# Moving the operands of a split-precision transformer kernel inside SBUF, and gating its merge stages in place

## The reference, cut to what matters

```python
# first stack, per layer: h = modulated rms_norm(x)
qa, ka, va, qb, kb, vb, ga, gb = split_in_proj(h @ w_in[l])
ya = window_attention_latent(...); yb = full_attention_latent(...)
m = jax.nn.sigmoid(ga) * (ya @ w_pa) + jax.nn.sigmoid(gb) * (yb @ w_pb)
x = x + gt1 * (m @ w_o)
x = x + gt2 * ((jax.nn.silu(h2 @ w_gate) * (h2 @ w_up)) @ w_down)
# second stack, per layer: three branches (sparse latent, stick-breaking, mLSTM)
proj = jnp.einsum('bsgc,gcd->bsgd', branches, w_branch)
gates = jax.nn.sigmoid(merge.reshape(bsz, seq, N_BRANCHES, D_MODEL))
x = x + jnp.sum(gates * proj, axis=2) @ w_out
```

## Time and profile before

| what | value |
|---|---|
| median of 3 runs | 2070.12 us (2069.21 to 2071.9) |
| the profiled execution's own time | 2063.66 us |
| its span, first to last instruction | 2062.2 us |
| TensorE matmul busy | 1955.9 us (95%) |
| VectorE busy | 1073.1 us (52%) |
| ScalarE busy | 873.6 us (42%) |
| GpSimd busy | 311.3 us (15%) |
| mean granted TensorE clock | 0.979 |

### The profile page before, as it was taken

One profiled execution on the slowest core, in us unless ns is written; L12 is line 12 of the kernel. 1 busy time (PEld: TensorE's weight loads), 2 busy tenths in 40 slices (PEclk: granted clock), 3 DMA queues, 4 the chain that ended last, 5 costly groups with the idle time before them and its releaser, 6 DMA issues.

```text
span 2062.2 us, 30759 instructions
## 1 busy us (share of the span) xinstructions
PE 1955.9 (95%) x12540; PEld 1617.4 (78%) x12540; DVE 1073.1 (52%) x2021; ACT 873.6 (42%) x1520; POOL 311.3 (15%) x149
## 2 busy tenths in 40 slices
PE   6999999999999999989989999899999899999996
PEld 3765676868888888677889999888788898788986
DVE  4335655642111111347776556569547755864675
ACT  3213545433222222334555444446454544755452
POOL 0220222434444443310000000000000000000100
PEclk9999999999999999999999999899999999999998
DMA  8333311243223222633237565443333444232441
GB/s 339 138 134 109 133 62 52 85 176 138 92 87 107 93 92 82 235 121 128 80 132 247 174 201 172 149 138 108 133 113 123 144 150 163 97 132 103 133 134 52
DMA packets 76700, 272.28 MB, mean 132 GB/s; under 512 B 8208, under 2 KB 11536, under 8 KB 76560
## 3 DMA queue, kind: packets, MB, share of 16 engines
q1 hardware_dynamic: 74656, 266.37, 37.6%
q10 hardware_dynamic: 1904, 3.94, 0.5%
HBM read 269.23 MB, written 1.05 MB: 131 GB/s over the span
## 4 chain that ended last, share of the span: by engine, by line
PE 82%; DVE 7%; ACT 6%; issue 2%; DMA 2%; POOL 1%; SPq 0%; ACTq 0%; DVEq 0%
PE bank L891 23%; PE bank L893 21%; PE bank L892 21%; DVE low L1671 2%; PE bank L972 2%; ACT high L1282 2%; PE bank L1052 2%; PE bank L1083 2%; PE bank L1065 2%; DMA raw<-stream 2%; PE bank L1041 1%; PE bank L1013 1%; POOL few L1614 1%; PE bank L984 1%; PE bank L1173 1%
## 5 line engine op out<-in xcount | busy, mean ns | idle before, releaser
L891 PE MATMUL bank<-h,high 128*128 128x256 f32 (+1 forms) x2432 | 795.2, 327 | 20.8 <-issue 6.8
L892 PE MATMUL bank<-h,high 128*128 128x256 f32 (+1 forms) x2432 | 759.0, 312 | 0.0
L893 PE MATMUL bank<-h,low 128*128 128x256 f32 (+1 forms) x2432 | 758.4, 312 | 0.0
L891 PEld LDWEIGHTS bank<-h,high 128*128 128x128 f32 x2432 | 464.6, 191 | 113.4 <-issue 71.9
L1282 ACT ACTIVATE high<-raw 128x1024 fp32r<-128x1024 f32 x408 | 426.7, 1052 | 214.9 <-PE bank L893 212.3
L892 PEld LDWEIGHTS bank<-h,high 128*128 128x128 f32 x2432 | 466.6, 192 | 28.6 <-issue 1.7
L893 PEld LDWEIGHTS bank<-h,low 128*128 128x128 f32 x2432 | 464.4, 191 | 29.3
L1671 DVE TENSOR_TENSOR low<-raw,high 128x1024 fp32r<-128x1024 f32 x296 | 364.2, 1234 | 222.1 <-ACT high L1282 221.0
L1605 POOL TENSOR_TENSOR low<-raw,high 128x1024 fp32r<-128x1024 f32 x112 | 271.7, 2432 | 501.7 <-ACT high L1282 501.7
L1614 POOL TENSOR_TENSOR few<-few,halves 128x2 f32<-128x2 f32 (+2 forms) x27 | 26.9, 998 | 814.6 <-DVE few L1757 814.6
L1698 DVE TENSOR_TENSOR gt<-bank,gt 128x512 f32<-128x512 f32 (+1 forms) x44 | 24.5, 558 | 201.7 <-PE bank L893 201.7
(11 more groups left out here) (280 smaller groups left out, 2529.5 us busy)
## 6 DMA issues: line engine op xcount, KB each, us to landing
raw<-stream SPq DMA_DIRECT2D x504, 512.0 KB, 3.3
xc<-x_in SPq DMA_DIRECT2D x1, 1024.0 KB, 5.5
xc<-ctx_in SPq DMA_DIRECT2D x1, 1024.0 KB, 7.8
out<-xc ACTq DMA_DIRECT2D x1, 1024.0 KB, 4.5
cst<-consts ACTq DMA_DIRECT2D x1, 896.0 KB, 7.6
cst<-consts ACTq DMA_DIRECT2D x1, 704.0 KB, 4.8
ukw<-uk ACTq DMA_DIRECT2D x1, 512.0 KB, 6.3
uvw<-uv ACTq DMA_DIRECT2D x1, 512.0 KB, 7.2
```

What stands on the lines that cost most here:

```text
L891: mm(dst, wh, xh, start=start, stop=False)
L892: mm(dst, wh, xl, start=False, stop=False)
L893: return mm(dst, wl, xh, start=False, stop=stop)
```

## The change

It does four things. (1) The small tensors are put ahead of the big ones with 56 columns of filling, so that `raw`, `high`, `low` and all that lies behind them in layer 0 of the first stack begin at a multiple of 512 bytes. (2) Empty columns of 48 floats (192 bytes, `ODD`) are put ahead of the layer-1 tensors of the first stack and of all of the second stack; `h0`/`h1` get a second place for layer 1, over the first. By the sizes, the 512-token linear stages of layer 0 then have a difference of 0 between moving and loaded operand, V of layer 0 has 0, all 256-token linear stages and K of layer 1 have 192 (BR too), and V of layer 1, SV and MV have 320 as before. (3) Gated products are written over the gates (`G`, `MG`); `mt` and `prod` are gone. In the first stack the subtraction is a step of its own (`mixlo`), which for tile j-1 stands behind PA of tile j; in the second the first addition (`mix2`) stands behind the second branch's matmuls, and `mix3lo` right behind `mix3`. (4) O of the last layer and both O2 start with two tiles together, not three.

```diff
+ODD = 48
...
             o.run(o.linear("PA", l, j))
+            if j:
+                o.step("mixlo", l, j - 1)
             o.run(o.linear("PB", l, j))
             o.step("mix", l, j)
+        o.step("mixlo", l, KT - 1)
...
-            elif j == 2:
-                o.run(o.together([("O", l, i) for i in range(3)], evac))
+            elif j == 1:
+                o.run(o.together([("O", l, i) for i in range(2)], evac))
...
                 o.run(o.linear("BR", l, 3 * j + g))
+                if g == 1:
+                    o.step("mix2", l, j)
             o.step("mix3", l, j)
+            o.step("mix3lo", l, j)
...
-            elif j == 2:
-                o.run(o.together([("O2", l, i) for i in range(3)], evac))
+            elif j == 1:
+                o.run(o.together([("O2", l, i) for i in range(2)], evac))
...
-        raw = sb("raw", [P, SLOTS, BLK * P])
...
-        vec = sb("vec", [P, -(-VEC_N // 16) * 16])[:, 0:VEC_N]
+        vec = sb("vec", [P, VEC_N])
...
+        sb("filled", [P, 56])
+        raw = sb("raw", [P, SLOTS, BLK * P])
+        high = sb("high", [P, PAIRS, BLK * P], F32R)
+        low = sb("low", [P, PAIRS, BLK * P], F32R)
...
-        hh, hl = (sb(f"h{i}", [P, KT, ALLT], F32R, scope=block1) for i in range(2))
+        layer0 = ExitStack()
+        hh, hl = ([sb(f"h{i}", [P, KT, ALLT], F32R, scope=layer0)] for i in range(2))
+        layer0.close()
+        sb("apart", [P, ODD], scope=block1)
+        for i, h in enumerate((hh, hl)):
+            h.append(sb(f"h{i}_1", [P, KT, ALLT], F32R, scope=block1))
+        sb("apart_end", [P, P - ODD], scope=block1)
...
+            if l:
+                sb("apart1", [P, ODD], scope=block1)
             G[l] = sb(f"gates{l}", [P, 16, n], scope=scope)
...
         block2 = ExitStack()
+        sb("apart2", [P, ODD], scope=block2)
...
-                        if j:
-                            dve.wait_ge("mix", no["mix", l, j - 1])
-                        tt(mt[l][i][:, :], ps[:, 0:n], G[l][:, 8 * i + j, :], ALU.mult).then_inc(S["drained_dve"], 1)
+                        g = G[l][:, 8 * i + j, :]
+                        tt(g, ps[:, 0:n], g, ALU.mult).then_inc(S["drained_dve"], 1)
...
-                        if j >= 4:
-                            dve.wait_ge("mix3", no["mix3", l, (j - 4) // 3])
-                        tt(prod[l][j % 4][:, :], ps[:, 0:n], MG[l][:, 8 * g + jj, :], ALU.mult).then_inc(S["drained_dve"], 1)
+                        t = MG[l][:, 8 * g + jj, :]
+                        tt(t, ps[:, 0:n], t, ALU.mult).then_inc(S["drained_dve"], 1)
...
                 elif kind == "mix":
                     l, j = key
-                    a, b = mt[l]
+                    a, b = (G[l][:, 8 * i + j, :] for i in range(2))
                     dve.wait_ge(*drained["PB", l, j])
-                    tt(a[:, :], a[:, :], b[:, :], ALU.add).then_inc(S["mixed"], 1)
-                    dve.wait_ge("mixed", no[step])
-                    dve.wait_ge("mix_hi", no[step])
-                    tt(M[l][1][:, j, :], a[:, :], M[l][0][:, j, :].bitcast(F32), ALU.subtract).then_inc(S["mix"], 1)
+                    tt(a, a, b, ALU.add).then_inc(S["mixed"], 1)
+
+                elif kind == "mixlo":
+                    l, j = key
+                    dve.wait_ge("mixed", no["mix", l, j])
+                    dve.wait_ge("mix_hi", no["mix", l, j])
+                    tt(M[l][1][:, j, :], G[l][:, j, :], M[l][0][:, j, :].bitcast(F32), ALU.subtract).then_inc(S["mix"], 1)
...
+                elif kind == "mix2":
+                    l, j = key
+                    a, b = (MG[l][:, 8 * g + j, :] for g in range(2))
+                    dve.wait_ge(*drained["BR", l, 3 * j + 1])
+                    tt(a, a, b, ALU.add).then_inc(S["mixed2"], 1)
...
```

More of the change, by code:

```diff
@@ L693 @@
 weigh_b weigh weigh_w weigh_exp weigh_e weighed read read_out centre centred remember
-parts_hi parts gate3 prod mixed3 mix3_hi mix3
+parts_hi parts gate3 mixed2 mixed3 mix3_hi mix3
 dve_own act_own block2
@@ L733, in build @@
         gs = sb("gs", [P, N_LAYERS, 2, KT, 2])
+        sb("filled", [P, 56])
+        raw = sb("raw", [P, SLOTS, BLK * P])
+        high = sb("high", [P, PAIRS, BLK * P], F32R)
+        low = sb("low", [P, PAIRS, BLK * P], F32R)
+        banks = [ctx.enter_context(nc.psum_tensor(f"bank{i}", [P, 512], F32)) for i in range(8)]
+        ones = sb("ones", [P, P])
+        square_sum = sb("square_sum", [P, ALLT])
+        xc = sb("xc", [P, KT, ALLT])
+        tmp = [sb(f"tmp{i}", [P, 512]) for i in range(2)]
         silu_c = sb("silu_c", [P, KT, 32])
@@ L754, in build @@
             M[l] = [sb(f"M{i}_{l}", [P, KT, n], F32R, scope=merge) for i in range(2)]
-            mt[l] = [sb(f"mt{i}_{l}", [P, n], scope=merge) for i in range(2)]
             merge.close()
@@ L787, in build @@
             B[l] = [sb(f"B{i}_{l}", [P, 12, SEQ], F32R, scope=merge) for i in range(2)]
-            prod[l] = [sb(f"prod{i}_{l}", [P, SEQ], scope=merge) for i in range(4)]
             merge.close()
@@ L918, in moving @@
                 if stage == "O2":
-                    pe.wait_ge("mix3", no["mix3", l, k])
+                    pe.wait_ge("mix3", no["mix3lo", l, k])
                 else:
@@ L1387, in scalar_program @@
                     if name in ("n1", "n2"):
-                        dst, which = hh, 0 if name == "n1" else 1
+                        which = 0 if name == "n1" else 1
                         if name == "n2":
@@ L2130, in vector_program @@
                     tt(B[l][1][:, c, :], Z[l][:, c, :], B[l][0][:, c, :].bitcast(F32), ALU.subtract).then_inc(S["parts"], 1)
+                elif kind == "mix2":
[3 more added lines that the diff above has]
+                    tt(a, a, b, ALU.add).then_inc(S["mixed2"], 1)
                 elif kind == "mix3":
                     l, j = key
-                    a, b, c = (prod[l][(3 * j + g) % 4] for g in range(3))
+                    a, c = (MG[l][:, 8 * g + j, :] for g in (0, 2))
+                    dve.wait_ge("mixed2", no["mix2", l, j])
                     dve.wait_ge(*drained["BR", l, 3 * j + 2])
-                    own += 1
-                    tt(a[:, :], a[:, :], b[:, :], ALU.add).then_inc(S["dve_own"], 1)
-                    dve.wait_ge("dve_own", own)
-                    tt(a[:, :], a[:, :], c[:, :], ALU.add).then_inc(S["mixed3"], 1)
-                    dve.wait_ge("mixed3", no[step])
-                    dve.wait_ge("mix3_hi", no[step])
-                    tt(hl2[:, j, :], a[:, :], hh2[:, j, :].bitcast(F32), ALU.subtract).then_inc(S["mix3"], 1)
+                    tt(a, a, c, ALU.add).then_inc(S["mixed3"], 1)
+                elif kind == "mix3lo":
+                    l, j = key
+                    dve.wait_ge("mixed3", no["mix3", l, j])
+                    dve.wait_ge("mix3_hi", no["mix3", l, j])
+                    tt(hl2[:, j, :], MG[l][:, j, :], hh2[:, j, :].bitcast(F32), ALU.subtract).then_inc(S["mix3"], 1)
         tensor_program()
```

41 lines of the change are left out of this document (17 added, 24 removed).

## The result

| kernel | median (range, executions) | ratio to before, 95% interval |
|---|---|---|
| before | 2069.66 us (2066.43 to 2071.9, 4) | |
| changed | 2052.67 us (2044.53 to 2052.98, 4) | 0.991 [0.9882, 0.9938] |

The change gained 17.0 us, not 41.3. The profiled execution took 2044.53 us (span 2043.0, mean granted clock 0.977), the three others 2052.37 to 2052.98. Against the profiled execution of before it gains 19.1 us.

What follows compares the result with a forecast made beforehand. TensorE's distance between matmul starts was taken to bound layer 0 of the first stack, from queries to FFN. 33 + 3.5 + 4.8 = 41.3 us off the median 2070.1 gave 2028.8 us; 8-in-10 range 2011 to 2063.

Steps and rivals of the forecast that it cites:

- The 512-column period: Layer 0, first stack: 2592 matmuls at difference 0 fall from 233.3 to 220 ns, 34.5 us, 33 after attention gives back 1.5.
- twice the better 256-column period: A bound on the 512-column matmul at difference 0: 226.6 ns, a gain of 6.7 ns each, 17.4 us.
- columns over clock: Lower end for the 512-column matmul at difference 0: 213.3 ns, a gain of 20.0 ns each, 51.8 us.
- The geometry that I gave: Reason for 220 ns: from 0, meetings of moving and loaded operand fall to the load's edge; from 192, in its middle.
- Merge of layer 1: First stack: VectorE's tile falls from 3.61 to 2.86 us, so TensorE's waits of 3.5 us go.
- BR: Second stack's BR stage: VectorE goes on setting it, so nothing gained, between +2.4 and -1 us.
- O2: Start of O2: the stop moves to the last merge step, behind 14 products; 2.4 us, twice, 4.8 us.
- 256-column streams: Matmuls of 256 columns kept at 192 bytes: 113.3 and 117.8 ns both go on, nothing gained.
- The rival of the slower period: Second stack's linear stages apart from BR go from 113.3 to 117.8 ns: 16.0 us more, 2044.8 us, chance 0.12.

Runs made afterwards that it cites:

- placement alone: The kernel before with the change's placement but its own merge steps (one layer-0 `mt` shares space with `hsq`): 2058.8 us, 0.9951 of before.
- the sweep: Matmul streams alone, no kernel compared and no ratio: moving operand shifted 0 to 992 bytes against the loaded one; 512 columns took 226.7 ns at 0, 233.3 to 234.2 at 192.
- merges only: The kernel before with the change's merge steps and two tiles together, at the addresses of before: 2063.65 us, 0.9972 of before.
- Loop cut: The changed kernel with ScalarE's rounding of a merge tile and VectorE's subtraction one tile later, also in BR: 2031.54 us, 0.9818 of before.
- three together: The changed kernel with three tiles of O and O2 together again, as before the change: 2056.85 us, 0.9947 of before.

## Why the prediction was wrong, step by step

The sum had three terms: 33 us from the addresses, 3.5 from the merge of layer 1, 4.8 from O2. The first came to 13.5 us in the stages that it named and to 9.9 in the time of placement alone, the second to nothing, the third to 6.2.

**The 512-column period was mis-sized; this is the largest miss.** That the place of the operands sets the period is shown by the sweep, and 0 is the right place. But it is 226.7 ns and not 220. Of the bounds that I had, "twice the better 256-column period" (226.6) was the true value, and I took the middle between it and columns over clock, which nothing has reached. 2592 x 6.6 = 17.1 us instead of 34.5. Even of these not all came: FFN 10.5, Q, PA, PB and O 3.0, which is 13.5; G's 384 matmuls took 98.0 us before and 98.2 now. They stand in short pieces between the attention's own matmuls. By the starts in the two traces, the 300 or so of them that stand close behind one another fell only from 233.2 to 231.1 ns on average (in a piece the first lie 224 to 236 ns apart, and about 227 only behind those); the 81 or so ahead of another kind of matmul stayed at 325 to 326 ns, and 3 now ran at the lower clock, 427 ns. The stretch of the attention became 0.8 us longer at the same work, and from the start to G some 2.8 us were lost. Neither can be put down to the placement: in merges only, with the addresses of before, G begins 4.4 us later than before and the attention is 1.2 us longer. Between 126 and 136 us the granted clock (third figure from the end) was 1.00 in the kernel before and 0.66 in the changed kernel and in merges only, in this order:

```profile
126.00:136.00 10.00, 9.81 (x62) 6.28 (x62) 1.79 (x8) 1.86 (x3) 5.13 (x3) 1.00 0.73 245
126.00:136.00 10.00, 10.00 (x48) 5.63 (x48) 1.58 (x6) 1.23 (x2) 3.31 (x2) 0.66 0.44 149
126.00:136.00 10.00, 8.75 (x43) 4.80 (x42) 1.13 (x6) 1.94 (x3) 3.94 (x2) 0.66 0.42 140
```

Placement alone measured 9.9 us, not 33. The geometry that I gave (loads meeting the moving operand at the edge) fits 0 as the best place for 512, but it would have made 0 good for 256 columns too, where it gives 120.0: it falls.

By the Trainium skill, page SBUF — State Buffer, section "Who interferes with whom", the moving operand and the weight loads have independent ports. Operands that never disturb each other would give one period, and the sweep disagrees with that: with the same instructions and only the address moved, 226.7 to 234.2 ns and 113.3 to 120.0. What inside the memory meets, no run here shows.

**Merge of layer 1: the step failed.** I said that VectorE "keeps two products, one split, an addition and a subtraction" and loses its 0.55 us of waiting, 3.61 to 2.86 us. It still took 3.61 to the hundredth. The 0.55 us was a symptom: shortened to 0.22, it came back as 0.73 us ahead of the split. I had read the idle time in front of one instruction as its price, and had not followed the loop through ScalarE, whose queue holds the rounding of the sum ahead of the next `high`. The kernel before had the same loop, and its trace shows it. Timeline of the kernel before, the tile of the earlier trace rows, VectorE, then ScalarE, which stands idle for 1.63 us until the addition is done; addition to addition is again 3.61 us.

```profile
1048.59 0.42 DVE L1941 TENSOR_TENSOR mt<-mt 128x256 f32<-128x256 f32 x1
...
1052.20 0.42 DVE L1941 TENSOR_TENSOR mt<-mt 128x256 f32<-128x256 f32 x1
...
1049.04 0.42 ACT L1454 ACTIVATE M<-mt 128x256 fp32r<-128x256 f32 x1 [1.63 <-DVE mt L1941]
1049.36 0.71 ACT L1449 ACTIVATE gates<-gates 128x256 f32<-128x256 f32 x2
1049.98 1.05 ACT L1282 ACTIVATE high<-raw 128x1024 fp32r<-128x1024 f32 x1
```

The change moved only VectorE's half. The 3.5 us didn't come; PA to O of layer 1 even lengthened by 1.3 us here and by 1.9 in merges only. Loop cut shows that this loop was the limit: the tile falls to 2.71 us with the same instructions.

**BR: the number right, the reason wrong.** It stayed at 38.5 us as forecast. But "VectorE goes on setting BR" is false: with the loop cut BR takes 33.9 us, and VectorE does its same work faster. It was a loop of the same kind: VectorE waited there for ScalarE both ahead of the split and ahead of the subtraction. The experiment moved the rounding and the subtraction at once, so it doesn't say how much each is worth.

**O2: right.** The wait went from the split to the last merge step (L2166), behind 14 products, as said. Timelines of the changed kernel there, TensorE and VectorE, in place of the earlier trace rows:

```profile
1634.97 0.28 PE L909 MATMUL bank<-h,low 128*128 128x256 f32 x1
1637.31 0.38 PE L907 MATMUL bank<-h,high 128*128 128x256 f32 x1 [2.06 <-DVE h L2166]
...
1636.83 0.43 DVE L2166 TENSOR_TENSOR h<-mg,h 128x256 fp32r<-128x256 f32 x1 [0.55 <-ACT h L1602]
```

It gained 3.0 and 3.2 us a layer against 2.4: the stop is 1.0 us shorter, and the 24 or so matmuls that ran at the lower of the two clocks before (213 ns apart) now run at the granted 1.00. Part of that is the clock's and not the order's: three together had a stop of 2.7 us in layer 0 without a slow matmul behind it, and took 1.4 us more than two together there. Merges only measures 5.0 us; its stages have 6.2 from O2, and PA to O of layer 1 takes 1.9 back.

**256-column streams: the sum right, the spread missed.** I kept 113.3 and 117.8 "as now", stage by stage. A stage doesn't always keep its period from one execution to the next: the FFN of layer 1 had 113.3 ns in one trace of the changed kernel and 117.8 in the other, which alone is 6.6 us. The rival of the slower period was real in parts (X and DQ of layer 1 went from 113.3 to 117.8 in the changed trace). Whether the change did that is open: they had 117.8 in both traces of the changed kernel and in placement only, 113.3 before and in merges only. V of layer 0 went from 117.8 to 119.9 as 0 gives, 0.2 us.

**The sum over the two profiled executions,** 2063.66 - 2044.53 = 19.1 us: 512-column streams 13.5, O2 6.2, the luckier period in the FFN of layer 1 6.6; against it PA, PB and O of layer 1 1.3, K, V and G of layer 0 1.0, and 4.9 left over in the second stack's periods, the start and the rest. By medians: 9.9 + 5.0 = 14.9 of the 17.0.

**Open.** What chooses between the two periods when a stream begins; why 112 always gives the faster; why the start and the attention lose 3 us or so, with the new addresses and with the old ones; which stages beyond O2 make three together slower.

## What to carry to other kernels

Follow a stage's period once round through every engine's queue before pricing a wait in it: the idle time in front of one instruction is not what its removal brings, and a step moved on one engine only leaves the loop whole. If the price of a change in TensorE's stream isn't in the trace, the best period that any stream of the trace holds was here a better estimate than a middle drawn to columns over clock. Where streams of fp32r matmuls with a weight load each bound a kernel, measure their period against the difference of the two addresses within 256 bytes, and behind several pauses, before placing the tensors.

## What the runs showed of the hardware that was not expected

- The period depends on the difference of the moving and the loaded operand's addresses modulo 256 bytes: 226.7 to 234.7 ns at 512 columns, 113.3 to 120.0 at 256, at a granted clock of 1.00. The best place for 512 columns, 0, is one of the slowest for 256. With the operands exchanged, the difference of moving minus loaded still decides (228.9 at 64, 233.3 at 192).
- A 256-column stream can have more than one steady period at one and the same difference, chosen by its beginning. Behind pauses of varied length it had 113.3 ns at 192 bytes in 16 of 22 beginnings and 117.8 in the others, at 64 in 2 of 22, at 0 never (120.0), and at 112 it had 113.3 to 114.0 in 10 of 10. The same beginning gave the same period: four times out of four in the first sweep, at 64 and at 192.
- Executions of one program on one core spread, 2044.53 to 2052.98 us side by side, and one stage at the other period makes 6.6 us between two traces. A difference of a few microseconds between two profiled executions can be this alone.
